# Two-block transformer kernel, first block: opening, rotation tables and turned root reordered, and in both output projections part of the low parts made by VectorE between the modulation rows, whose loads GpSimd asks for

## The reference, cut to what matters

```python
y = rms_norm(h, mix_norm[i])
proj = y @ w_in[i]          # x_lru, g_lru, q, k, v, g_ret, u_sgu, v_sgu, g_sgu
lru_out = rg_lru(causal_depthwise_conv(x_lru, ...), ...)
ret_out = retention(q, k, v, positions, ret_norm[i])     # rope from positions
sgu_out = spatial_gating(u_sgu, v_sgu, ...)
mixed = concatenate([lru_out * silu(g_lru), ret_out * silu(g_ret), sgu_out * silu(g_sgu)])
h = h + mixed @ w_out[i]                                  # 2048 -> 1024
z = rms_norm(h, ple_norm[i])
h = h + sigmoid(z @ w_ple_gate[i]) * (p[i] @ w_ple_proj[i])
```

## Time and profile before

| | |
|---|---|
| median of 3 runs | 2577.36 us (2576.5 to 2580.62) |
| profiled execution, its own time | 2576.13 us |
| its span | 2574.3 us |
| PE busy | 2428.7 us (94%) |
| DVE busy | 2052.4 us (80%) |
| ACT, POOL busy | 1319.4 us (51%), 763.7 us (30%) |

### The profile page before, as it was taken

One profiled execution on the slowest core, in us unless ns is written; L12 is line 12 of the kernel. 1 busy time (PEld: TensorE's weight loads), 2 busy tenths in 40 slices (PEclk: granted clock), 3 DMA queues, 4 the chain that ended last, 5 costly groups with the idle time before them and its releaser, 6 DMA issues.

```text
span 2574.3 us, 31318 instructions
## 1 busy us (share of the span) xinstructions
PE 2428.7 (94%) x10763; PEld 1941.1 (75%) x10763; DVE 2052.4 (80%) x1804; ACT 1319.4 (51%) x1206; POOL 763.7 (30%) x400
## 2 busy tenths in 40 slices
PE   7799999799999999998968999999999999999995
PEld 5577788676777887785656888888888888888884
DVE  6668589566685777787147999999999999999994
ACT  3342232333422325424135777777777777777772
POOL 3334258233342583242212112211221212211220
PEclk9899999799999999999968999999999999999997
DMA  6232234422322382121028999999999999999992
GB/s 215 82 100 88 74 123 163 156 66 90 99 89 74 129 289 66 59 92 39 1 109 306 368 379 367 373 368 371 374 365 370 366 380 364 372 363 372 377 358 99
DMA packets 104490, 572.47 MB, mean 222 GB/s; under 512 B 14192, under 2 KB 14336, under 8 KB 54352
## 3 DMA queue, kind: packets, MB, share of 16 engines
q1 hardware_dynamic: 93696, 540.32, 55.8%
q0 software_dynamic: 10288, 30.76, 4.9%
q10 hardware_dynamic: 432, 0.40, 0.1%
HBM read 559.37 MB, written 24.12 MB: 227 GB/s over the span
## 4 chain that ended last, share of the span: by engine, by line
PE 83%; DVE 9%; DVEq 3%; DMA 2%; ACT 2%; issue 1%; ACTq 1%; POOL 0%; SPq 0%; POOLq 0%
PE ps L1469 80%; PE ps L1134 2%; DVE scr L2307 2%; DVEq L2309 1%; DVE scr L2152 1%; DVE y_split L2089 0%; DMA scr<-in_ada 0%; PE ps L642 0%; DVE mix L2199 0%; DMA pieces<-in_pieces 0%; DVE scr L2197 0%; DMA scr<-in_positions 0%; DMA mix<-acc_rows 0%; DVEq L2405 0%; ACTq L1843 0%
## 5 line engine op out<-in xcount | busy, mean ns | idle before, releaser
L1261 DVE TENSOR_TENSOR w_split<-raw,w_split 128x2048 fp32r<-128x2048 f32 x386 | 877.5, 2288 | 54.4 <-ACT w_split L1213 43.5
L1469 PE MATMUL ps<-y_split,pieces_split 128*128 128x512 f32 x3600 | 847.3, 396 | 49.2 <-POOL pieces_split L2485 18.0
L1213 ACT ACTIVATE w_split<-raw 128x2048 fp32r<-128x2048 f32 x386 | 736.1, 1916 | 197.6 <-PE ps L1469 177.9
L1469 PEld LDWEIGHTS ps<-y_split,pieces_split 128*128 128x128 f32 x3600 | 681.9, 190 | 202.3 <-issue 58.5
L1469 PE MATMUL ps<-w_split,rows_T 128*128 128x512 f32 x3096 | 753.5, 394 | 1.9 <-DVE rows_T L1267 1.9
L1469 PEld LDWEIGHTS ps<-w_split,rows_T 128*128 128x128 f32 x3096 | 576.6, 189 | 119.7 <-DVE rows_T L1267 2.5
L2485 POOL TENSOR_TENSOR pieces_split<-pieces,pieces_split 128x1024 fp32r<-128x1024 f32 x171 | 430.3, 2525 | 698.8 <-ACT pieces_split L1794 580.3
L1794 ACT ACTIVATE pieces_split<-pieces 128x1024 fp32r<-128x1024 f32 x144 | 151.4, 1058 | 456.4 <-PE ps L1469 389.3
L1469 PE MATMUL ps<-w_split,hidden_T 128*128 128x512 f32 x1536 | 363.3, 392 | 0.2 <-DVE hidden_T L1267 0.2
L1469 PEld LDWEIGHTS ps<-w_split,hidden_T 128*128 128x128 f32 x1536 | 285.8, 188 | 70.5 <-DVE hidden_T L1267 12.0
L1325 POOL COPY rows_i<-slot_tokens 128x1 int32 (+1 forms) x34 | 59.5, 1751 | 403.4 <-PE ps L1134 369.3
(11 more groups left out here) (260 smaller groups left out, 2063.9 us busy)
## 6 DMA issues: line engine op xcount, KB each, us to landing
raw<-in_w_moe SPq DMA_DIRECT2D x386, 1024.0 KB, 7.4
pieces<-in_pieces SPq DMA_DIRECT2D x181, 512.0 KB, 3.5
scr<-in_ada SPq DMA_DIRECT2D x48, 512.0 KB, 4.4
scr<-in_ple SPq DMA_DIRECT2D x2, 1536.0 KB, 6.8
acc_rows<-in_zeros POOLq DMA_DIRECT2D x5, 512.0 KB, 11.5
hT<-in_xT SPq DMA_DIRECT2D x8, 256.0 KB, 8.5
h_rows<-scr SPq DMA_DIRECT2D x4, 512.0 KB, 2.6
mix<-acc_rows SPq DMA_DIRECT2D x4, 512.0 KB, 5.1
```

The costliest lines, as they stand in the source:

```text
L1213: nc.scalar.activation(wsp[:, p % SPLIT, 0], raw[:, p % RAW, :], ACT.Copy).then_inc(high, 3 if p == 1 else 1)
L1261: nc.vector.tensor_tensor(wsp[:, p % SPLIT, 1], raw[:, p % RAW, :], wsp[:, p % SPLIT, 0].bitcast(F32), ALU.subtract).then_inc(low, 3 if p ...
L1469: return pe.matmul(out, lhsT, rhs, start=start, stop=stop)
```

## The change: what it does

1. Opening. SP loads piece 0, then all of x, then the other pieces. ACT has its table loaded by a dummy copy, waits for `par` alone, copies piece 0, then makes all eight input highs, then the other pieces' highs and the squares. DVE makes the low of piece 0, then all eight input lows, then the sums of squares. In layer 0 PE runs xl0 alone in `side_by_side`, then xl1 and xl2 as ordinary pieces, then the sum of squares, into the bank of gl3, then gl0 and on. Pool A loses its extra opening turn. Positions are loaded by POOL, among the constants.
2. Rotation tables. The angles move from ahead of the gates gl1 to gl5 to behind them: cosine's behind the gates, sine's behind the three `la` operations. The sines on ACT move behind the roots of the first recurrence.
3. `rT`, in both layers: ACT copies it right after the tanh of r and i, ahead of the exp and tanh pairs, and the `ahead("gl5")` between is gone.
4. Modulation rows: layer 0 takes groups 0 and 1 (16 rows, two operations each), layer 1 groups 2 to 5 (32 rows, one each): 64 operations before and after. POOL asks for the loads, into three slots in layer 0 and five in layer 1.
5. DVE makes the lows of wo.6 to wo.15 and of mixed tiles 5 to 15, with 1 to 3 rows behind each pair.

```diff
+ADA_RAW = (3, 5)
+ADA_J = ((0, 1), (2, 3, 4, 5))
...
+OWN_LOWS = range(6, 16)
+ADA_TURN = ([3] + [1, 1, 2, 1, 1, 2, 1, 1, 2, 1], [5] + [3, 3, 2, 3, 3, 2, 3, 3, 2, 3])
...
             for n in range(A_RAW):
-                if n < 3:
-                    sp.dma_start(pieces[:, n, :], io["pieces"][n]).then_inc(p_in[n], 16)
-                for kt in range(n, n + 1) if n < 2 else range(2, DK) if n == 2 else ():
+                sp.dma_start(pieces[:, n, :], io["pieces"][n]).then_inc(p_in[n], 16)
+                for kt in range(DK) if n == 0 else ():
                     sp.dma_start(hT[:, kt, :], io["xT"][kt * P:(kt + 1) * P, :]).then_inc(x_in[kt], 16)
...
-                side_by_side(A, ("xl0", "xl1", "xl2"), 0, opening_sum)
-                for name, _, pool, g in LAYER[3:12]:
+                first = ("xl0", "xl1", "xl2") if layer else ("xl0",)
+                side_by_side(A, first, 0, opening_sum)
+                for name, _, pool, g in LAYER[len(first):12]:
+                    if layer == 0 and name == "gl0":
+
+                        pe.wait_ge(sq_added, 1)
+                        mm(ps[:, V.bank("gl3"), :], ones[:], sq_sum, True, True).then_inc(first_sum, 1)
                     project(pools[pool], g)
...
-            act.wait_ge(par_in, 48)
+            act.wait_ge(warm, 1)
+            nc.scalar.activation(small[:, 1:2], small[:, 0:1], ACT.Copy)
+            act.wait_ge(par_in, 16)
+            first_high(0)
             for k in range(DK):
-                if k < 3:
...
                 act.wait_ge(x_in[k], 16)
                 gained_high(k, 0, "mix_norm")
...
-                if layer == 0:
-                    prep_sin()
...
-                    ahead("gl5" if g == 0 else "gr1")
+                    if g == 0:
+                        nc.scalar.activation(rT, full(A, "rt")[:, 0:8], ACT.Copy)
+                        act.drain().then_inc(A.free, 1)
+                    else:
+                        ahead("gr1")
...
                     if g == 0:
+                        if layer == 0:
+                            prep_sin()
                         ahead("gr0")
...
                 if layer == 0:
-                    prep_angles()
-                gates([f"gl{i}" for i in range(1, 6)], lambda i: 1 + i, 1)
+                    prep_positions()
+                    prep_angles(rcos, 0.25)
...
+                at_ = iter(range(ADA_N[layer]))
+                for _ in range(ADA_TURN[layer][0]):
+                    ada_row(next(at_))
+                for k, turn_ in zip(OWN_LOWS, ADA_TURN[layer][1:]):
+                    own_mixed_low(k - 1)
+                    own_low(f"wo.{k}")
+                    for _ in range(turn_):
+                        ada_row(next(at_))
+                own_mixed_low(15)
...
+                def ada_load(i):
+                    slot, _ = ada_landed(layer, i)
+                    if i >= ADA_RAW[layer]:
+                        pool.wait_ge(ada_used, ADA_FIRST[layer] + i - ADA_RAW[layer] + 1)
+                    pool.dma_start(aring[slot], io["ada"][ADA_FIRST[layer] + i]).then_inc(ada_in[slot], 16)
...
                     k = n - L_AT["wo.0"] - A_SPLIT
-                    for tile in range(4) if k == 0 else [k + 3] if 0 < k < 13 else []:
+                    if k == 0:
+                        pool.wait_ge(V.full, V.done(layer, "o5"))
+                        for i in range(ADA_RAW[layer]):
+                            ada_load(i)
+                    for tile in range(4) if k == 0 else [4] if k == 1 else []:
                         mixed_low(layer * 16 + tile + 1, tile % DK, tile)
-                    low_part_of(layer * NS + n + 1, n, *((layer, L_SPLIT[n]) if n < NS else (layer + 1, n - NS)))
+                    if n == first_own:
+
+                        for i in range(ADA_RAW[layer], ADA_N[layer]):
+                            ada_load(i)
+                        pool.wait_ge(p_low, layer * NS + last_own + 1)
+                        pool.wait_ge(mixl, layer * 16 + 16)
+                    if not first_own <= n <= last_own:
+                        low_part_of(layer * NS + n + 1, n, *((layer, L_SPLIT[n]) if n < NS else (layer + 1, n - NS)))
```

More of the change, by code:

```diff
@@ L117, with ada_landed @@
 assert L_SPLIT[:A_SPLIT] == T_SPLIT[:A_SPLIT] == list(range(A_SPLIT))
-ADA_RAW, ADA_N = 3, 3 * DK
-ADA_WHO = [((0, 1), (0, 1), (0,)), ((0,), (0,), (0,))]
-ADA_AT = [[(j, who) for j in range(3) for who in ADA_WHO[layer][j]] for layer in range(L)]
-ADA_LOADS = {"wo.2": 3, **{f"wo.{k}": min(3 + 2 * (k - 4), 3 * DK) for k in range(5, 16)}}
+ADA_RAW = (3, 5)
+ADA_J = ((0, 1), (2, 3, 4, 5))
+ADA_WHO = {0: (0, 1), 1: (0, 1), 2: (0,), 3: (0,), 4: (0,), 5: (0,)}
+ADA_AT = [[(j, who) for j in ADA_J[layer] for who in ADA_WHO[j]] for layer in range(L)]
+ADA_N = [len(ADA_J[layer]) * DK for layer in range(L)]
+ADA_FIRST = [0, ADA_N[0]]
+OWN_LOWS = range(6, 16)
+ADA_TURN = ([3] + [1, 1, 2, 1, 1, 2, 1, 1, 2, 1], [5] + [3, 3, 2, 3, 3, 2, 3, 3, 2, 3])
+assert all(sum(ADA_TURN[layer]) == ADA_N[layer] for layer in range(L))
+def ada_landed(layer, i):
+    slot = i % ADA_RAW[layer]
+    before = len(range(slot, ADA_N[0], ADA_RAW[0])) if layer and slot < ADA_RAW[0] else 0
+    return slot, 16 * (before + i // ADA_RAW[layer] + 1)
 PC = {}
@@ L410, in build @@
         part_used = sem("piece_part_used")
-        ada_in = [sem(f"ada_in{i}") for i in range(ADA_RAW)]
+        ada_in = [sem(f"ada_in{i}") for i in range(max(ADA_RAW))]
         ada_used, ada_ready = sem("ada_used"), sem("ada_sums")
@@ L1698, in modulation @@
                         for c in range(DK):
-                            m = mm(out[:, i * DK + c:i * DK + c + 1], adasum[i][:, c * P:(c + 1) * P], ones[:, 0:1],
+                            m = mm(out[:, i * DK + c:i * DK + c + 1], adasum[layer][i][:, c * P:(c + 1) * P], ones[:, 0:1],
                                    True, True)
@@ L1800, in full @@
                     return ps[:, pool.bank(g), :]
-                norm_root(A, layer - 1, "next")
-                if layer == 0:
+                if layer:
+                    norm_root(A, layer - 1, "next")
+                else:
+                    act.wait_ge(first_sum, 1)
+                    nc.scalar.activation(rn, ps[:, V.bank("gl3"), :], ACT.Sqrt, bias=EPSC, scale=1.0 / D)
+                    act.drain().then_inc(root_ready, 1)
                     prep_exp()
@@ L1840, in _ @@
                         nc.scalar.activation(mix[:, 9 + m, :], mix[:, 9 + m, :], ACT.Tanh).then_inc(at_ready, 1)
-                    if g == 0:
-                        nc.scalar.activation(rT, full(A, "rt")[:, 0:8], ACT.Copy)
-                        act.drain().then_inc(A.free, 1)
                     ahead("v0.3" if g == 0 else "v1.1")
@@ L2124, in _ @@
                 norm_inverse(2 * layer + 1)
+                if layer == 0:
+                    dve.sem_inc(V.free, 1)
                 def scale_gate(g, n):
@@ L2167, in _ @@
                 conv(5)
+                gates([f"gl{i}" for i in range(1, 6)], lambda i: 1 + i, 1)
                 if layer == 0:
-                    prep_angles()
-                gates([f"gl{i}" for i in range(1, 6)], lambda i: 1 + i, 1)
+                    prep_positions()
+                    prep_angles(rcos, 0.25)
                 for g in range(2):
@@ L2177, in _ @@
                                                 ALU.mult).then_inc(la_ready, 1)
+                    if layer == 0 and g == 0:
+                        prep_angles(rsin, 0.0)
+                        dve.sem_inc(prep_v, 1)
                     for m in range(3):
@@ L2297, in _, with ada_row @@
                 dve.drain().then_inc(mix_ready, 1)
[L2299 to L2303 removed]
+                def ada_row(i):
+                    j, k = ADA_J[layer][i // DK], i % DK
+                    slot, at_ = ada_landed(layer, i)
+                    dve.wait_ge(ada_in[slot], at_)
+                    for who in ADA_WHO[j]:
+                        out, c = adasum[layer][ADA_AT[layer].index((j, who))], cond[:, k, who:who + 1]
```

143 lines of the change are left out of this document (68 added, 75 removed).

## The result

The change makes the kernel faster: 2533.26 us (median of 4 runs, 2531.95 to 2534.4) against 2577.85 (4 runs, 2576.5 to 2580.62), ratio 0.9826 with a 95% interval of 0.9808 to 0.9843. The forecast was 2533.5. The profiled execution took 2532.86 for a span of 2531.0.

A forecast was written before the change was run, and what follows sets the result against it. PE, busy 94% of the span, was taken as the bound, so only its idle or slow time could be won. Gains of 19.6, 13.4 and 18.2 less costs of 6.3 and 1.0 gave 43.9 us: 2533.5, range 2527 to 2550.

The forecast's parts named there:

- What bounds the kernel: PE busy 94%; four waits: 18.0 us at opening, 11.6 before gl5, 4.9 twice behind rT's copy, 15.4 behind layer 0's wo.
- Opening and angles, 19.6: Start to gl5, layer 0: earlier PE start and angles off the gates' path win 19.6 us (15 to 21.8).
- The half of the slow matmuls that I counted as won: gl5's 24 matmuls took 7.69 us instead of 5.46; half of the 2.2 was counted, since a shorter stall remains.
- the opening gives half: Opening: POOL's lows collide with DVE's input lows and sums, sum of squares at 33, term 10: 2543 us; chance 0.1.
- rT, 13.4: v0, both layers: waits of 4.8 and 4.9 us go, plus 1.85 per layer of slow matmuls: 13.4 (9.7 to 13.4).
- Cover in the recurrence: The moved angles hide in DVE's 11.37 us wait for ACT's roots, of which some 5 us stay as cover.
- Output projection of layer 0, 18.2: wo, layer 0: the 15.4 us stall goes and 34 matmuls return from 10.55 to 7.7 us: 18.2 won.
- The costs, minus 6.3 and minus 1: POOL's requests before both wo, 4.8 us plus 1.5 for the clock (3 to 8); layer 1's later hT start, 1.
- rows end 75 us in: wo, layer 1: behind wo.6's high at 17 us, DVE's lows and 27 rows end 75 us after the start.
- the first rival: wo, layer 1: row loads asked for by POOL are slow, at 11.5 us hT starts 5 late: 2539 us; chance 0.18.
- Modulation matmuls move, nothing: 16 modulation matmuls move from layer 0 to layer 1, at no net cost.
- The sum: Whole kernel: 19.6 + 13.4 + 18.2 - 6.3 - 1.0 = 43.9 us won, forecast 2533.5 us.
- My price for it: wo: twelve two-port operations, eight in layer 0, four in layer 1, each hold a request 1.28 us: 15 us, 2549.

## Why the prediction was right, point by point

- **What bounds the kernel**: the four waits were the gain. PE's waits up to 1250 us lost the four entries, and putting back two of them put back their time. For the opening the load of positions was only the first link of what ended last: PE waited for a low of POOL's, and the load alone explains 3.4 of the 10.4.
- **Opening and angles, 19.6**: PE started at 7.57 (said 7.5), the reciprocal at 27.96 (27.5), gl5 at 73.89 (73.6) behind a wait of 3.09 (3 or less). The half of the slow matmuls that I counted as won was not: gl5's 24 took 7.26 of 7.69. The blocks of r and i start 18.7 earlier (80.99 against 99.66). The rival "the opening gives half" didn't come, yet its mechanism is there: three convolutions took 8.32, 6.38 and 4.36 us for three operations that take 2.40 undisturbed, 11.9 us in all beside POOL's lows, but the same was so before.
- **rT, 13.4**: no wait is left, and the size was right: from the start of v0 to the end of its 96 matmuls layer 0 takes 6.7 us less than before (21.9 against 28.6), and layer 1 6.8 less by v1. Putting the copy back cost 13.8 in these stretches, though only 11.5 to 12 by the time of the whole.
- **Cover in the recurrence**: DVE still waits 5.92 us for the roots in layer 0; about 5 was said.
- **Output projection of layer 0, 18.2**: with the requests out of the way, start of wo to sum of squares is 103.1 against 121.0, so 18.0. In the changed kernel it is 16.4, since wo starts at the lower clock there.
- **The costs, minus 6.3 and minus 1**: the mechanism was right and both were too small. Moving the first requests gave back 7.9 in the traces, 4.6 of it the two waits (4.8 said) and 3.2 the slow starts behind them, for which I had 1.5; the medians give 9 to 10, just beyond my bound of 8. In layer 1 hT starts 86.6 us in, 4.0 later than before, not 1, and this costs PE 2.4. The step that failed is "rows end 75 us in": they ended at 79.4. wo.6's high came at 20.3 and not at 17, since PE had gone through the first pieces at the lower clock (DVE makes that low 17.7 us in where the first requests are moved), and DVE waited 5.9 us for rows 5 to 7, which POOL could only ask for behind its own lows, 17 us into wo; against that DVE's work took 53 us where I had 57. It is the first rival in small: not slow loads, but late requests.
- **Modulation matmuls move, nothing**: layer 0 won 4.1 (80 in 14.60 before, 64 in 10.48) and layer 1 lost 4.2 (48 in 6.92, then 64 in 11.15). The net is nothing; it is no small thing at either place.
- **The sum**: 43.3 on the span (2574.3 - 2531.0), 43.9 said. That it is so near is partly luck. When PE comes to the context, behind all that the change touches, 40.6 us are won (1042.57 against 1001.96): 0.9 less than said in the opening and 2.9 more of costs account for the 3.3 that are missing, within 0.5. The rest of the 43.3 comes in the attention, which both kernels do alike: from the context to the projection behind the attention the kernel before took 204.4 us and the changed one 201.2, but over all twelve traces this stretch takes 201.2 to 204.4, whatever the edits, and 202.8 in the second trace of the changed kernel.

The rule of the Trainium skill that I weighed, that a two-port VectorE operation locks out the writing of descriptors ("SBUF — State Buffer", "SBUF: two separate sides"), isn't tested here: in the trace of the changed kernel no request of POOL's in either wo overlaps one of the TENSOR_SCALAR rows (the nearest is 0.29 us off). My price for it was too high besides: layer 0 has four such operations and not eight, so eight in all, about 10 us and not 15. A request takes 0.53 us on the mean, and 8 x 0.53 = 4.2 of the 4.6 us by which the waits ahead of wo grew are those requests. What decides the row operations stands on the same page: "Who interferes with whom" says that a VectorE instruction with two SBUF inputs contends with a GpSimd instruction that reads SBUF, and that one of them then fully blocks for the whole of the other. This case's trace agrees: 3.61 where 1.22 is free, ending 1.10 after POOL's operation.

Not tried: asking for the rows from SP with the lows on DVE (a row's slot comes free only behind lows that need later pieces of SP's queue, which could lock up), and DVE making lows beside its convolutions.

## What to carry to other kernels

A 128x1024 operation of POOL beside a DVE that is busy with two-input operations costs DVE about 2.1 us of standing still (28 us for 13 additions), more than the 1.22 that it takes DVE to make a piece's low itself. In wo of layer 0 before the change the price was less for each and shared: 40 row operations took some 40 us more than undisturbed beside 30 lows of POOL's, and POOL's piece lows took 2.85 us where 2.40 is free. So work is moved off POOL not because POOL is slow but because DVE pays for it. And a load request in an engine's queue counts as work of that engine at that place: three and five requests of 0.53 us at the start of the two wo cost 7.9 us in the traces with the clock behind them (9 to 10 by the medians), and add no wait of PE three pieces earlier.
